# First MLP product: two plain row tiles and fifteen pairs in place of four and fourteen, with the half sums taken kind by kind

## What is computed

```python
def finish_layer(x, pool_out, attn_out, w_out, ln2, w_ff1, w_ff2):
    h = x + jnp.einsum('bte,ed->btd', jnp.concatenate([pool_out, attn_out], axis=-1), w_out)
    a = jnp.square(jax.nn.relu(jnp.einsum('btd,df->btf', rmsnorm(h, ln2), w_ff1)))
    return h + jnp.einsum('btf,fd->btd', a, w_ff2)
```

## Time and profile before

| what | value |
| --- | --- |
| time, median of 3 runs | 1308.26 us (1307.36 to 1312.16) |
| the profiled execution: its own time | 1312.98 us |
| its span (first to last instruction) | 1310.6 us |
| PE / DVE / ACT / POOL busy | 98% / 63% / 45% / 36% of the span |
| plain tiles of the first product | from 611.79 us to 667.25 us |
| the fourteen pairs | from 667.25 us to 952.69 us |

### The profile page before, as it was taken

One profiled execution on the slowest core, in us unless ns is written; L12 is line 12 of the kernel. 1 busy time (PEld: TensorE's weight loads), 2 busy tenths in 40 slices (PEclk: granted clock), 3 DMA queues, 4 the chain that ended last, 5 costly groups with the idle time before them and its releaser, 6 DMA issues.

```text
span 1310.6 us, 25941 instructions
## 1 busy us (share of the span) xinstructions
PE 1278.3 (98%) x10008; PEld 1181.7 (90%) x10008; DVE 823.8 (63%) x1711; ACT 592.1 (45%) x1099; POOL 474.1 (36%) x555
## 2 busy tenths in 40 slices
PE   5999999999999999999999999999999999999998
PEld 4958999996666899878999999999999999999997
DVE  5368998776985232217853443433447979879985
ACT  6445788746876422324633333333322233332444
POOL 5433985441331231132166767767630000000300
PEclk9999999998999999999999999999999999999999
DMA  6340113310001777694242332323480240512103
GB/s 197 76 113 17 45 46 116 98 50 1 2 2 33 235 239 221 199 309 143 72 126 81 129 107 91 123 82 124 145 313 1 98 164 1 198 64 98 35 1 133
DMA packets 140289, 141.72 MB, mean 108 GB/s; under 512 B 20889, under 2 KB 98841, under 8 KB 140160
## 3 DMA queue, kind: packets, MB, share of 16 engines
q1 hardware_dynamic: 121669, 116.31, 28.1%
q10 hardware_dynamic: 17842, 21.94, 4.6%
q0 software_dynamic: 656, 1.84, 0.6%
HBM read 111.87 MB, written 26.50 MB: 106 GB/s over the span
## 4 chain that ended last, share of the span: by engine, by line
PE 82%; DVE 6%; ACT 1%; issue 1%; DVEq 0%; ACTq 0%
PE bank L2362 75%; PE bank L2553 3%; PE bank L2652 2%; DVE junk L1813 1%; PE bank L2607 1%; ACT sjunk L1215 1%; PE bank L2410 1%; DVE hl_lo L2170 1%; DVE acc L2216 0%; DVE cc_lo L1893 0%; DVE hid_lo L2163 0%; PE bank L2579 0%; PE bank L2906 0%; DVE lack L1817 0%; DVE hn_lo L2041 0%
## 5 line engine op out<-in xcount | busy, mean ns | idle before, releaser
L2362 PE MATMUL bank<-bo_hi,ao_hi 128*128 128x264 f32 x672 | 191.3, 285 | 0.0
L2362 PE MATMUL bank<-bo_hi,ao_lo 128*128 128x264 f32 x672 | 191.1, 284 | 0.0
L2362 PE MATMUL bank<-bo_lo,ao_hi 128*128 128x264 f32 x672 | 190.7, 284 | 0.0
L2362 PE MATMUL bank<-xn_hi,w_hi 128*128 128x384 f32 (+1 forms) x456 | 151.0, 331 | 0.0
L2362 PE MATMUL bank<-xn_lo,w_hi 128*128 128x384 f32 (+1 forms) x456 | 147.6, 324 | 0.0
L2362 PE MATMUL bank<-xn_hi,w_lo 128*128 128x384 f32 (+1 forms) x456 | 147.2, 323 | 0.0
L792 POOL TENSOR_TENSOR w_hi<-w_raw,zero 128x256 fp32r<-128x256 f32 x108 | 68.9, 638 | 198.9 <-PE bank L2362 183.0
L2362 PE MATMUL bank<-hi_T,hn_hi 128*128 128x264 f32 x448 | 127.7, 285 | 0.0
L2362 PE MATMUL bank<-lo_T,hn_hi 128*128 128x264 f32 x448 | 127.1, 284 | 0.0
L2362 PE MATMUL bank<-hi_T,hn_lo 128*128 128x264 f32 x448 | 127.0, 283 | 0.0
L2362 PEld LDWEIGHTS bank<-bo_hi,ao_lo 128*128 128x128 f32 x672 | 126.6, 188 | 0.0
(11 more groups left out here) (322 smaller groups left out, 3482.4 us busy)
## 6 DMA issues: line engine op xcount, KB each, us to landing
page<-in_cache_k_dram SPq DMA_DIRECT2D x64, 256.0 KB, 3.6
page<-in_cache_v_dram SPq DMA_DIRECT2D x64, 256.0 KB, 3.4
hidden_dram<-stg ACTq DMA_DIRECT2D x56, 264.0 KB, 2.0
b<-hidden_dram SPq DMA_DIRECT2D x12, 1056.0 KB, 7.4
a<-in_w_ff_dram SPq DMA_DIRECT2D x12, 1024.0 KB, 5.3
w_raw<-in_w_ff_dram SPq DMA_DIRECT2D x22, 512.0 KB, 5.1
w_raw<-in_w_in_dram SPq DMA_DIRECT2D x18, 512.0 KB, 3.7
wr<-in_w_ff_dram SPq DMA_DIRECT2D x14, 512.0 KB, 4.7
```

The source lines that it names most:

```text
L2362: return nc.tensor.matmul(out, lhsT, rhs, start=start, stop=stop)
```

## The change

Two plain row tiles are left (`FU` = 2), the pairs are 15. P2 comes second in a pair, ahead of P7. The six plain pieces stand in banks 0 to 5, one each, in the order (0,0) (0,1) (1,1) (0,2) (1,2) (1,0), and the products of all pairs go round the four bank pairs (6,7), (0,1), (2,3), (4,5). `half_sums(k)`, which made all four sums of one block, becomes `half_sum(n)`, which makes the four blocks of one sum, in the order T3, T2, T1, T4; high and low parts follow kind by kind as well, and PE waits for each kind apart. ACT splits no plain weights any more (`act_high`). At the end, the hidden tiles of `down` are asked for ahead of its weights, and these wait until the low sums of the last pair are done, since the last of fifteen pairs stands in `w_raw`.

```diff
-    NPR = (DFF // P - FG) // 2
-    PRODS = ["P1", "P7", "P6", "P5", "P2", "P4", "P3"]
+    FU = 2
+    N_DN = N_FF + FU
+    NPR = (DFF // P - FU) // 2
+    PRODS = ["P1", "P2", "P7", "P6", "P5", "P4", "P3"]
...
-        for i, g in first_tiles:
-            take(("up", i, g), 3 * (i % 2) + g)
-        bp, yp, xp_, dp = (6, 7), (1, 2), (4, 5), (0, 3)
+        for q, (i, g) in enumerate(first_tiles):
+            take(("up", i, g), q)
+        pairs = ((6, 7), (0, 1), (2, 3), (4, 5))
         for pr in range(NPR):
-            for name, pair in zip(PRODS, (bp, yp, xp_, dp, bp, dp, bp)):
+            for i, name in enumerate(PRODS):
                 for s in range(2):
-                    take((name, pr, s), pair[s])
-            bp, yp, dp = yp, dp, bp
+                    take((name, pr, s), pairs[(7 * pr + i) % 4][s])
...
-            sp.wait_ge(s_slo, 7 * (NPR - 1))
+            stored_upto(FG)
+            for s in range(2):
+                wait_full(sp, ("P7", NPR - 1, s))
+            for k in (0, 2):
+                hidden_in(hraw, 0, k, s_hd[k // 2])
+            sp.wait_ge(s_slo, 7 * NPR)
             for i in range(FG):
-                down_load(0, i, N_FF + FG, 0)
+                down_load(0, i, N_DN, 0)
...
                 sum_low(pr, 0, a11)
-                sum_low(pr, 1, a21)
-                pool.wait_ge(s_slo, 7 * pr + 2)
+                sum_low(pr, 1, a12)
+                sum_low(pr, 2, a21)
+                pool.wait_ge(s_slo, 7 * pr + 3)
                 nc.gpsimd.tensor_tensor(a21, a22, a21, ALU.subtract).then_inc(s_ws_, 1)
                 pool.wait_ge(s_ws_, 4 * pr + 2)
                 nc.gpsimd.tensor_tensor(a11, a21, a11, ALU.add).then_inc(s_ws_, 1)
-                sum_low(pr, 2, a21)
+                sum_low(pr, 3, a21)
...
-                    wait_full(act, ("up", 3, 2))
+                    wait_full(act, ("up", 1, 2))
...
+            for blk in range(3):
+                sum_high(blk)
+            half_high("T3")
             for q in range(3):
                 square(q)
...
+            half_high("T2")
+            sum_high(3)
+            half_high("T1")
             square(3)
+            half_high("T4")
             square(4)
...
-                if n >= 7 * NPR - 4 and name in ("P5", "P4"):
-                    hidden_high(range(2) if name == "P5" else range(2, FG))
-                    if name == "P4":
-                        w_high(N_FF + FG + 1)
+                if n >= 7 * NPR - 4 and name in ("P6", "P5"):
+                    hidden_high(range(2) if name == "P6" else range(2, FG))
+                    if name == "P5":
+                        w_high(N_DN + 1)
...
-            half_sums(0)
+            half_sum("T3")
+            half_sum("T2")
             for q in range(3):
                 first_out(q)
...
+            half_low("T3")
+            half_sum("T1")
+            first_out(3)
+            half_sum("T4")
+            half_low("T2")
+            first_out(4)
+            first_out(5)
+            half_low("T1")
+            half_low("T4")
...
-                    if pr == 0 and i == 1:
-                        pe.wait_ge(s_tl, 4 * HK)
+                    if pr == 0 and 2 <= i <= 5:
+                        pe.wait_ge(s_tl, (i - 1) * HK)
```

More of the change, by code:

```diff
@@ L687, in down_load @@
                 sp.dma_start(dst, wf2[s, i]).then_inc(s_w[n % 2], 16)
-            for i in range(2, FG):
-                up_load(0, i, N_FF, 0)
             for pr in range(NPR):
                 if pr == 0:
-                    sp.wait_ge(s_wlo, N_FF + FG)
+                    sp.wait_ge(s_wlo, N_DN)
                 elif pr == 1:
-                    wait_full(sp, ("up", 2, 0))
-                    wait_full(sp, ("up", 3, 0))
+                    wait_full(sp, ("up", 0, 2))
+                    wait_full(sp, ("up", 1, 0))
                 else:
@@ L704, in stored_upto @@
             def stored_upto(n):
-                stores = 3 * FG + 2 * (n - FG)
+                stores = 3 * FU + 2 * (n - FU)
                 for k in range(3):
@@ L1020, in after_tile @@
                 return full[b], u + 1
-            for i in range(FG):
+            for i in range(FU):
                 if i == 1:
                     pool.wait_ge(s_nl, 2 * KC)
-                ff_split(block_no(N_FF + i), after_tile(("proj", N_FF + i - 2, 2)) if i < 2 else after_tile(("up", i - 2, 2)))
+                ff_split(block_no(N_FF + i), after_tile(("proj", N_FF + i - 2, 2)))
             def a_part(pr, c, h):
@@ L1060, in _ @@
                 if i < 2:
-                    last, low = (s_slo, 7 * NPR), (s_cmb, 10 * NPR - (4 if i == 0 else 0))
+                    last, low = (s_slo, 7 * NPR), (s_cmb, 10 * NPR - (7 if i == 0 else 0))
                 else:
                     last = after_tile(("dn", 0, 2 * (i - 2) + 1, 2))
-                ff_split(block_no(N_FF + FG + i), last, low)
+                ff_split(block_no(N_DN + i), last, low)
             for i in range(FG):
@@ L1468, in half_gain, with half_high @@
                 nc.scalar.activation(t_f["T4"][:, k, :], acc[:, k, HT:T], ACT.Identity, scale=g2[:, k:k + 1]).then_inc(s_t12, 1)
-            def half_high(k):
-                for i, n in enumerate(("T3", "T1", "T2", "T4")):
-                    act.wait_ge(s_tf, 4 * k + i + 1)
+            def half_high(n):
+                for k in range(HK):
+                    act.wait_ge(s_tf, HK * ("T3", "T2", "T1", "T4").index(n) + k + 1)
                     nc.scalar.activation(t_hi[n][:, k, :], t_f[n][:, k, :], ACT.Copy).then_inc(s_th, 1)
@@ L1481, in sum_high @@
                 else:
-                    wait_full(act, ("up", 3, 2))
+                    wait_full(act, ("up", 1, 2))
                 c = slice(HT + P * (blk % 4), HT + P * (blk % 4) + P)
-                part, half, sums = ((0, 0, 0), (1, 0, 1), (1, 0, 2), (0, 0, 3), (0, 1, 0), (1, 1, 0), (1, 0, 4))[i]
+                part, half, sums = ((0, 0, 0), (0, 1, 0), (1, 0, 1), (1, 0, 2), (0, 0, 3), (1, 1, 0), (1, 0, 4))[i]
                 act.wait_ge(s_raw[2 * (pr % 2) + part], 16 * (pr // 2 + 1))
@@ L1553, in _ @@
             h_spread(2)
-            w_high(N_FF + 2, ("up", 0, 2))
+            for blk in range(3):
+                sum_high(blk)
+            half_high("T3")
             for q in range(3):
                 square(q)
-            half_high(0)
-            half_high(1)
+            half_high("T2")
+            sum_high(3)
+            half_high("T1")
             square(3)
+            half_high("T4")
             square(4)
-            w_high(N_FF + 3, ("up", 1, 2))
             square(5)
-            half_high(2)
-            half_high(3)
-            for q in range(6, 9):
-                square(q)
-            for blk in range(4):
-                sum_high(blk)
-            for q in range(9, 12):
-                square(q)
             for n in range(7 * NPR):
```

84 lines of the change are left out of this document (35 added, 49 removed).

## The result

The changed kernel takes 1321.39 us in the median (1320.11 to 1321.77, 4 runs), beside 1308.16 us for the kernel before on the same chip. The ratio is 1.0089, with a 95% interval of 1.0071 to 1.0107: slower by 13.2 us, where 10.8 were forecast. The profiled execution took 1321.03 us, its span 1319.2 us at a granted clock of 0.995.

What follows compares the result with a forecast made beforehand. The prediction took PE's own work as the bound (busy 98%). Its terms, -2.84 + 11.7 + 0.5 + 1.4 = +10.8 us, on a median of 1308.26 gave 1319 us, own range 1315 to 1323, wider range 1310 to 1326.

Steps and rivals of the forecast that it cites:

- a shared door: DVE instructions with two SBUF tensors and POOL instructions never run together; where both have work, they take turns.
- The work saved: After six plain tiles, a fifteenth pair (20.39 us) replaces six plain pieces (23.23 us): 2.84 us gained without waits.
- P7 5.4 and P6 3.1 late: First pair: DVE reads bank 3 late, delaying P7 5.4 us, then banks 4 and 5, delaying P6 3.1 us.
- the prediction's own sign: Check on the changed profile's first pair: if P7 starts by 651 us, the assumed DVE and POOL turns were wrong.
- P5 0.8: First pair: P5 waits 0.8 us for the fifth weight sum, behind the last two squares, and its low part.
- its low part on POOL waits its turn with DVE: First pair, ahead of P5: the fifth weight sum, ready 663.3, gets its low part on POOL at 664.9 us.
- P4 2.2 and P3 0.1: First pair: P4 waits 2.2 us for P2's reading behind DVE's low parts; P3 waits 0.1 us for weights.
- All waits: PE's waits in the first pair, P7 through P3, summed to 11.7 us.
- Clock: First pair: waits lower PE's granted clock, costing 0.5 us, bounds 0 and 2.9; slow products mostly hide in later waits.
- The end: Start of `down`: late `w_raw` load makes PE wait 2.5 us, 1.1 given back; net +1.4, bounds -1.1 and +3.5.
- no turns at the door: First pair: DVE and POOL don't hold each other up; 2.8 us lost, 2.84 saved, total 1309.7 us; chance 10%.
- Milder turns: First pair: DVE keeps the door while busy; P7 near 651, P6 near 656, some 6 us lost; chance 10%.

Runs made afterwards that it cites:

- e5: Kernel before (four plain tiles, fourteen pairs, early load) with only the new product order, bank round and hidden low parts a product earlier; 1306.81 us, ratio 0.9985.
- e2: Changed kernel with POOL's weight sums and low parts in the first pair cut to 4 columns of 128; 1314.05 us, ratio 1.0040.
- e8: Changed kernel with a tiny DVE fill (0.06 us) behind each low part of T1 and T4 in the first pair; 1320.28 us, ratio 1.0067.
- e7: The three mends of e6 plus 48 unused filler matmuls into P6's bank ahead of P6 in the first pair; 1319.26 us, ratio 1.0069.
- e1: Changed kernel with DVE reading plain tiles of banks 3, 4 and 5 ahead of the T1 sums; 1320.8 us, ratio 1.0091.
- e3: Changed kernel with the first weights of `down` loaded between the two loads of `hraw`; 1320.18 us, ratio 1.0082.
- e6: Changed kernel with the edits of e1, e3 and e4 together; 1317.26 us, ratio 1.0060.
- e9: The three mends of e6 plus the tiny DVE fills of e8; 1317.43 us, ratio 1.0059.
- e4: Changed kernel with ACT making the fifth weight sum's high part ahead of the last two squares; 1318.35 us, ratio 1.0069.

## Why the prediction was right, step by step

The range held the time, and the cause is the one that it named: the half sums lose their cover, and DVE's list, stretched by POOL at a shared door, is late for the first pair. e5 shows that the order of the products costs nothing; e2 and its timelines put 6 to 7 of the 9 us of waits at the door. Two of the four terms came out above their own upper bounds, the clock and the end. Of the terms:

- **The work saved, -2.84.** Right: pairs two to fifteen take 20.37 us each, before 20.39.
- **P7 5.4 and P6 3.1 late.** Measured 2.9 and 4.1. P7's first piece began on time, since its bank had long been read; only the second stood behind bank 3. So 1.45 us of the 5.4, a piece's length, were a wrong reading of which bank each piece needs. The rest is that DVE was through sooner: bank 3 was read 10.1 us after P1's start, where 11.1 was forecast. By the prediction's own sign, a P7 that starts by 651, the turns would have been wrong; P7's first piece did start 5.9 us after P1, 649.9 on the forecast's clock, and the turns were there all the same. The sign rested on the wrong bank. P6 took up most of what P7 didn't wait, and began 15.8 us after P1, forecast 17.3. Its two limits fell together: T2's last low part ended at 654.9 us, the reading of P6's first bank behind it at 655.3.
- **P5 0.8.** Measured 2.1, though both neighbours came sooner. The step that failed is "its low part on POOL waits its turn with DVE": POOL had no turn until DVE's eight low parts were through, 3.95 us where 1.6 had been put.
- **P4 2.2 and P3 0.1.** Measured 0, by the same mistake with the other sign. DVE's low parts of T1 and T4 were not held up, and ended 21.1 us after P1's start instead of 24.7.
- **All waits, 11.7.** Measured 9.0. Had the turns been kept everywhere, P4 would have waited and P5 less; e8, whose gaps bring the turns back, has just that.
- **Clock, 0.5 (bounds 0 and 2.9).** The term that was mis-sized: 3.1 us in the profile, above the upper bound. The argument that a slow product ends in another's wait held for one place: e7 shows it for P6. It doesn't hold for the sum of the kernel, whose clock falls in two stretches of 3.4 us here and for up to 10.2 us in a row in the profiles of e1, e3 and e6. The Trainium skill (TensorE: Matmul & The Clock Gate, "Why this matters for your kernels") warns that an idle gap between bursts of matmuls drops the clock back to half. By that rule this trace agrees: the granted clock fell at 655.2 us, at the end of the wait ahead of P6, and at 662.0, right behind the wait ahead of P5.
- **The end, 1.4 (bounds -1.1 and 3.5).** Measured 3.8. The wait is 3.7 instead of 2.5, since `w_raw` landed 9.3 us after P7's end (945.9 us), past the late bound of 8.4, and POOL then took 2.5 and 3.2 us where 1.9 and 2.4 had been put; and the clock fell behind the wait, 1.6 us (matmuls of 384 columns at 0.32 us in place of 0.176), a cost that this term didn't hold at all. What was given back is 1.5 us, not 1.1 (e5's `down` has no waits).

The terms thus miss by -2.7, +2.6 and +2.4 us, and together by 2.4. That the first two cancel is luck.

The rival "no turns at the door" falls by the timeline (four low parts in 6.76 us). "Milder turns" has the mechanism that held P5: DVE kept the door while it had work, and POOL's sum was pushed behind. It is nearer at P7 (1.2 us late, measured 2.9, forecast 5.4), but not at P6, which it has 12 us after P1 (measured 15.8, forecast 17.3), and its price, 6 us, leaves out the clock and the wait at the end. What stays open: how the chip decides whom to serve. A gap of DVE is enough to let POOL in (e8, e9), but between 645 and 649 us POOL got between DVE's half sums without one, and in e4 once between two low parts.

## What to carry to other kernels

Ask of a faster algorithm what the plain work in front of it was covering: here 2.84 us less of PE's work took away 23 us of plain tiles under which DVE could prepare, and the kernel became 13.2 us slower. A wait that ends at a bank reading is not cured by moving the reading when the engine's list is full up to that point; the windows row with 10.00 of 10 us says so before any experiment. A load on which the next stage waits goes ahead of the large ones in its queue, as far as its buffer allows: in e3 it took 3.1 of 3.7 us off the wait for one moved line. And the engine that a list of waits names is worth a second look: in e2 it named a low part of DVE, where those that PE needed had been done for over 2.5 us, and the true one was the same door again.
